# The down weights of an expert loop issued from ScalarE's queue instead of the first queue

## The chip, the cores and the metric

The kernel runs on one core of a Trainium2 chip. A core has TensorE (PE, matrix products; its weight loads are shown as PEld), VectorE (DVE), ScalarE (ACT), GpSimd (POOL) and SyncE (SP), each with a queue of its own, semaphores between them, and 16 DMA engines that carry what the queues issue. The metric is the device time of one execution in microseconds.

## The reference, cut to what matters

Two layers over 256 tokens of width 1024, all float32. Each layer is a mixer, a layer norm, a mixture of experts and another layer norm:

```
x = LN(alpha*x + mixer(x));  x = LN(alpha*x + MoE(x))
MoE(x): scores = sigmoid(x @ w_router)            # 64 experts, top 8 of each token
        routed = sum over chosen e of gate_e * (silu(x @ w_gate[e]) * (x @ w_up[e])) @ w_down[e]
        MoE = routed + (silu(x @ ws_gate) * (x @ ws_up)) @ ws_down
```

Of an expert, w_gate and w_up are 1024 x 256 and w_down is 256 x 1024, so each is 1 MiB; the 64 experts of a layer have 192 MiB, and each byte of them is read once.

## The kernel before, in words

The expert part works through 32 pairs of experts, four pairs (p = 0 to 3) to an octet, eight octets to a layer. For each octet the tokens of eight experts are gathered into columns by matmuls (L1916). For each pair PE runs `pe_pair`: gates and ups of both experts (L1945, 16 steps of two), half of the scatter of the pair before (L1995), the transposes of the hidden values and of the token map (L1967 to L1979), the other half of that scatter, for p = 3 the gather of the next octet, and the two halves of the down product (L1987). ACT (`act_pair`) makes silu (L2182), copies the token map (L2189), and for p = 3 half of the gathered columns, then waits for each half of the down product and copies it to `y_parts` as the high part (L2204). DVE makes the hidden product (L2276), its copy (L2282) and the low part (L2302).

The weights lie in five slots. Slots 0 and 1 (in `RING`) serve p = 0, slots 2 and 3 (in `AR`) serve p = 1 and p = 3, and p = 2 uses slot EX and slot 1 (EX has its gate and up weights in the first part of `RING` and its down weights in `GB`, where the norms' weights lie otherwise). A slot's gate and up part is free when `gate_up_done` says so, its down part when `down` does. In the last octet p = 2 uses slots 0 and 1, not EX.

All loads are issued by SP, in one written order, in `loads`. `load_experts(pair, experts)` waits for `gate_up_done` of the pair two before, issues the gate and up weights of its experts (`load_gate_up`, L1796 and L1797), waits for `down` of the same pair, and issues the down weights (`load_down`, L1800). In the first four octets the experts 8i+5 and 8i+8 go together, then 8i+6 and 8i+7, then 8i+9 and 8i+12, then 8i+10 and 8i+11. From the fifth octet on, `load_octet` takes 8i+8 after 8i+6 and 8i+7, and 8i+12 after 8i+10 and 8i+11. `load_last_pair` loads the last two experts, with the ups on a semaphore of their own. Behind it SP issues, in layer 0, the first weights of the next mixer (`load_rw`, into the places of slot EX, read by L1437), and in both layers the weights of the norm (`load_ln`, into `GB`, L459 and L460; in layer 1 first read by L422). PE waits for `gu_w[slot]` before a pair's gates and ups, and for `dn_w[slot]` before its down product.

Of the kernel before, what the change touches and what calls it, by code (L numbers as in the profile page):

```python
# [23 lines left out]
E = 64  # L24
# [9 lines left out]
PAIRS = E // 2  # L34
OCTS = E // 8
EX = 4
# [44 lines left out]
def program(nc, a):  # L81
    ctx = ExitStack()
    with ctx:
# [3 lines left out]
        def sem(name):  # L87
            return ctx.enter_context(nc.semaphore(name))
# [785 lines left out]
        def load_rw(sp, src, c):  # L874
            sp.dma_start(RWC[c].rearrange("p (k c) -> p k c", k=KT), src[:, :, c * CB:(c + 1) * CB]).then_inc(s_rw[c], 16)
# [663 lines left out]
        def pe_core(pe):  # L1539
# [231 lines left out]
        moe_shared = {n: sem("moe_" + n) for n in per_layer} | {  # L1771
            "gu_w": [sem(f"gate_up_loaded{s}") for s in range(EX + 1)],
            "dn_w": [sem(f"down_loaded{s}") for s in range(EX + 1)]}
        uses = [OCTS + 1, E // 4, E // 4, E // 4, OCTS - 1]
        gate_ups = [32 * n - (16 if s in (2, 3) else 0) for s, n in enumerate(uses)]
        once_an_octet = (0, EX)
        per_layer |= {"map_copied": PAIRS, "gates_ready": PAIRS, "turned": PAIRS + 1}
# [2 lines left out]
        def moe_view(l):  # L1780

            q = moe_shared | {n: sem(f"l{l}_{n}") for n in over_names}
            past = {n: l * count for n, count in per_layer.items()}
# [10 lines left out]
            def load_gate_up(sp, e, slot):  # L1794
                g, u, d = wslot(slot)
                sp.dma_start(g, gate_src(wg, e)).then_inc(q["gu_w"][slot], 16)  # L1796
                sp.dma_start(u, gate_src(wu, e)).then_inc(q["gu_w"][slot], 16)  # L1797

            def load_down(sp, e, slot):
                sp.dma_start(wslot(slot)[2], down_src(wd, e)).then_inc(q["dn_w"][slot], 16)  # L1800

            def load_expert(sp, e, slot):
                load_gate_up(sp, e, slot)
                load_down(sp, e, slot)
# [9 lines left out]
            def loads(sp):  # L1814
                sp.wait_ge(s_res, 2 * TT * st)
                if l == 0:
                    load_expert(sp, 0, 0)
                load_expert(sp, 2, 2)
                if l:
                    load_expert(sp, 3, 3)  # L1820
                g, u, d = wslot(EX)
                sp.wait_ge(s_ln, TT * (l + 1))
                load_down(sp, 4, EX)
                sp.wait_ge(q["shared_gate"], 1 + past["shared_gate"])
                sp.dma_start(g, gate_src(wg, 4)).then_inc(q["gu_w"][EX], 16)
                sp.wait_ge(q["shared_gate_up"], 1 + past["shared_gate_up"])
                sp.dma_start(u, gate_src(wu, 4)).then_inc(q["gu_w"][EX], 16)

                def load_experts(pair, experts):

                    sp.wait_ge(q["gate_up_done"], pair - 1 + past["gate_up_done"])
                    for e, s in experts:
                        load_gate_up(sp, e, s)
                    sp.wait_ge(q["down"], 2 * (pair - 1) + past["down"])
                    for e, s in experts:
                        load_down(sp, e, s)

                def load_last_pair():

                    sp.wait_ge(q["gate_up_done"], PAIRS - 2 + past["gate_up_done"])  # L1840
                    for e, s in ((E - 2, 2), (E - 1, 3)):
                        sp.dma_start(wslot(s)[0], gate_src(wg, e)).then_inc(q["gu_w"][s], 16)
                    for e, s in ((E - 2, 2), (E - 1, 3)):
                        sp.dma_start(wslot(s)[1], gate_src(wu, e)).then_inc(q["shared_and_last_ups_loaded"], 16)
                    sp.wait_ge(q["down"], 2 * (PAIRS - 2) + past["down"])
                    for e, s in ((E - 2, 2), (E - 1, 3)):
                        load_down(sp, e, s)

                def load_octet(i, twelfth):

                    load_experts(4 * i + 2, [(8 * i + 5, 1)])
                    load_experts(4 * i + 3, [(8 * i + 6, 2), (8 * i + 7, 3)])
                    load_expert(sp, 8 * i + 8, 0)
                    load_experts(4 * i + 4, [(8 * i + 9, 1)])
                    load_experts(4 * i + 5, [(8 * i + 10, 2), (8 * i + 11, 3)])
                    if twelfth == 0:
                        load_experts(4 * i + 6, [(8 * i + 12, 0)])
                    else:
                        load_expert(sp, 8 * i + 12, twelfth)

                sp.wait_ge(q["first_gates"], 1 + past["first_gates"])
                for e, s in ((5, 1), (8, 0)):
                    sp.dma_start(wslot(s)[0], gate_src(wg, e)).then_inc(q["gu_w"][s], 16)
                sp.wait_ge(q["gate_up_done"], 1 + past["gate_up_done"])
                for e, s in ((5, 1), (8, 0)):
                    sp.dma_start(wslot(s)[1], gate_src(wu, e)).then_inc(q["gu_w"][s], 16)
                sp.wait_ge(q["down"], 2 + past["down"])
                for e, s in ((5, 1), (8, 0)):
                    load_down(sp, e, s)
                load_experts(3, [(6, 2), (7, 3)])  # L1870
                load_experts(4, [(9, 1), (12, EX)])
                load_experts(5, [(10, 2), (11, 3)])
                with sp.Fori(1, 4) as i:
                    load_experts(4 * i + 2, [(8 * i + 5, 1), (8 * i + 8, 0)])
                    load_experts(4 * i + 3, [(8 * i + 6, 2), (8 * i + 7, 3)])
                    load_experts(4 * i + 4, [(8 * i + 9, 1), (8 * i + 12, EX)])
                    load_experts(4 * i + 5, [(8 * i + 10, 2), (8 * i + 11, 3)])
                with sp.Fori(4, OCTS - 2) as i:
                    load_octet(i, EX)
                load_octet(OCTS - 2, 0)  # L1880
                load_experts(PAIRS - 2, [(E - 3, 1)])
                load_last_pair()
                if l == 1:
                    load_ln(sp, st)
                else:
                    for c in range(2):
                        load_rw(sp, w_key, c)
                    sp.wait_ge(q["gate_up_done"], PAIRS)
                    for c in range(2, 4):
                        load_rw(sp, w_key, c)  # L1890
                    load_ln(sp, st)
                sp.wait_ge(q["rank_ready"], 1 + past["rank_ready"])
                most = nc.sync.value_load(cnti[0:1, 2 * l:2 * l + 1], min_val=0, max_val=T)
                with sp.If(most > CAP):

                    sp.wait_ge(q["over_list"], 1)
                    rounds = nc.sync.value_load(cnti[0:1, 2 * l + 1:2 * l + 2], min_val=1, max_val=NOV // 2)
                    with sp.Fori(0, rounds) as i:
                        sp.wait_ge(q["over_free"], i + 1)
                        for s in range(2):  # L1900
                            e = nc.sync.value_load(elist[0:1, ds(2 * i + s, 1)], min_val=0, max_val=E - 1)
                            g, u, d = wslot(s)
                            sp.dma_start(g, gate_src(wg, e)).then_inc(q["over_loaded"], 16)
                            sp.dma_start(u, gate_src(wu, e)).then_inc(q["over_loaded"], 16)
                            sp.dma_start(d, down_src(wd, e)).then_inc(q["over_loaded"], 16)
# [154 lines left out]
            def pe_moe(pe):  # L2060
# [54 lines left out]
                    for p in range(4):  # L2115
                        pe_pair(pe, 4 * i + p, p, i, True, spare=(p == 2))
                for p in range(4):
                    pe_pair(pe, PAIRS - 4 + p, p, OCTS - 1, False, last=(p == 3))
                pe.wait_ge(q["rank_ready"], 1 + past["rank_ready"])
                most = nc.tensor.value_load(cnti[0:1, 2 * l:2 * l + 1], min_val=0, max_val=T)  # L2120
                for n, made in enumerate(("high", "low")):
# [69 lines left out]
            def act_pair(s, i, p, oct_, more, last=False):  # L2191
                s.wait_ge(q["gate_up_done"], i + 1 + past["gate_up_done"])
                silu(q["silu_ready"])
                if not last:
                    s.wait_ge(q["gates_ready"], i + 2 + past["gates_ready"])
                    s.wait_ge(q["scattered"], i + past["scattered"])
                    copy_map(s, 1 - p % 2)
                if p == 3 and more:
                    for n in range(1, KT, 2):
                        wait_gathered(s, n, oct_ + 1)  # L2200
                        copy_gathered(nc.scalar.copy, n, oct_ + 1).then_inc(q["odd_copied"], 1)
                for h in range(2):
                    s.wait_ge(q["down"], 2 * i + h + 1 + past["down"])
                    nc.scalar.copy(YS[:, 0, h * 512:(h + 1) * 512], PS[:, 5 + h, :]).then_inc(q["high"], 1)  # L2204

            def residual(n):

# [359 lines left out]
```

## Time and profile before

| | us |
|---|---|
| median of 3 runs | 1322.86 (1322.58 to 1324.11) |
| the profiled execution | 1321.67 |
| its span | 1319.8 |
| PE busy in the span | 1300.7 (99%) |
| DVE, ACT busy | 441.5, 264.6 |
| HBM read | 448.26 MB, 340 GB/s over the span |

The expert loops lie from about 134 to 594 us and from about 846 to 1306 us. A busy time is the time in which the engine had an instruction under way; the ends of matmuls are modelled, so a busy PE isn't PE at its peak. In the chain of waits, a piece named "issue" is time in which PE waited for nothing that this view names; a landing of a DMA can lie behind it. A line such as `L1945` is a line of the kernel, printed above for the functions of the change.

### The profile page before, as it was taken

How to read it: one execution, taken by the hardware profiler on the slowest of the kernel's cores; microseconds unless marked ns; L12 is line 12 of the kernel's file. 1: busy time of each engine (PE TensorE's matmuls, PEld its weight loads, DVE VectorE, ACT ScalarE, POOL GpSimd, SP SyncE). 2: the span in 40 equal slices, each digit the busy share in tenths (PEclk: the TensorE clock that was granted, in tenths of full speed). 3: DMA queues.
4: the chain of work that ended last, by engine and by line, in shares of the span. 5: the costliest groups of instructions: out<-in, count | busy, mean ns of one | idle time of the engine just before them, and what ended most of it. 6: DMA issues, size and time to landing. Idle time of an engine off the chain costs nothing.

```text
span 1319.8 us, 23498 instructions
## 1 busy us (share of the span) xinstructions
PE 1300.7 (99%) x9812; PEld 753.2 (57%) x9812; DVE 441.5 (33%) x960; ACT 264.6 (20%) x524; POOL 79.8 (6%) x122
## 2 busy tenths in 40 slices
PE   9999999999999999999999999999999999999997
PEld 8889444435534443449688998734444353444433
DVE  2245122222222222228663665422223122222213
ACT  1231211111111111113432330211111111111111
POOL 7302000000000000000002201100000000000001
PEclk9999999999999999999999999999999999999999
DMA  5697799999999999995543016799999999999994
GB/s 184 162 383 318 295 423 415 422 422 422 422 416 422 422 422 422 421 391 173 188 158 101 4 43 270 313 384 418 422 421 423 421 422 415 422 422 422 422 421 179
DMA packets 98824, 450.38 MB, mean 341 GB/s; under 512 B 16193, under 2 KB 45505, under 8 KB 49089
## 3 DMA queue, kind: packets, MB, share of 16 engines
q1 hardware_dynamic: 98752, 449.34, 84.6%
q8 instruction: 56, 0.92, 0.3%
q14 instruction: 16, 0.12, 0.0%
HBM read 448.26 MB, written 1.05 MB: 340 GB/s over the span
## 4 chain that ended last, share of the span: by engine, by line
PE 95%; DVE 3%; ACT 1%; issue 1%; POOL 0%; DVEq 0%; POOLq 0%
PE PS L1945 31%; PE PS L1987 17%; PE PS L1995 10%; PE PS L1916 7%; PE PS L536 4%; PE PS L498 3%; PE PS L1412 2%; PE PS L1437 2%; PE PS L1398 2%; PE PS L1959 2%; PE PS L1967 1%; PE PS L1575 1%; PE PS L521 1%; PE PS L1591 1%; PE PS L2002 1%; PE PS L2071 1%
## 5 line engine op out<-in xcount | busy, mean ns | idle before, releaser
L2302 DVE TENSOR_TENSOR y_parts<-PS,y_parts 128x512 fp32r<-128x512 f32 x128 | 88.5, 692 | 216.5 <-ACT y_parts L2204 216.5
L2276 DVE SCALAR_TENSOR_TENSOR AR<-AR,PS 128x256 f32<-128x256 f32 x64 | 30.7, 480 | 382.7 <-ACT AR L2182 382.7
L1995 PE MATMUL PS<-y_parts,token_map 128*128 128x512 f32 x496 | 146.5, 417 | 0.0
L1995 PEld LDWEIGHTS PS<-y_parts,token_map 128*128 128x128 f32 x496 | 83.5, 188 | 60.0 <-issue 49.4
L1987 PE MATMUL PS<-AR 128*64 128x512 f32 x512 | 116.9, 598 | 0.0
L1987 PE MATMUL PS<-RING,AR 128*64 128x512 f32 x400 | 116.8, 598 | 0.0
L1945 PE MATMUL PS<-RING,xT 128*64 128x512 f32 x480 | 108.2, 592 | 1.6 <-issue 1.6
L2204 ACT CAST y_parts<-PS 128x512 fp32r<-128x512 f32 x128 | 75.0, 586 | 171.9 <-PE PS L1987 171.9
L1945 PE MATMUL PS<-AR,xT 128*64 128x512 f32 x480 | 108.2, 592 | 1.0 <-issue 1.0
L1945 PE MATMUL PS<-AR 128*64 128x512 f32 x480 | 108.1, 592 | 0.0
L1945 PE MATMUL PS<-RING,AR 128*64 128x512 f32 x480 | 108.1, 592 | 0.0
L2182 ACT ACTIVATE AR<-PS 128x256 f32<-128x256 f32 x64 | 24.6, 385 | 399.6 <-PE PS L1945 380.3
L1916 PE MATMUL PS<-slot_map,x_high 128*128 128x384 f32 x256 | 86.4, 337 | 0.1
L1916 PE MATMUL PS<-slot_map,x_low 128*128 128x384 f32 x256 | 85.8, 335 | 0.0
L1945 PEld LDWEIGHTS PS<-RING,xT 128*64 128x64 f32 x480 | 34.7, 137 | 70.3 <-issue 70.3
L1945 PEld LDWEIGHTS PS<-AR,xT 128*64 128x64 f32 x480 | 34.7, 137 | 69.8 <-issue 69.8
L1945 PEld LDWEIGHTS PS<-AR 128*64 128x64 f32 x480 | 35.0, 137 | 68.0 <-issue 68.0
L1945 PEld LDWEIGHTS PS<-RING,AR 128*64 128x64 f32 x480 | 34.9, 137 | 68.1 <-issue 68.1
L1987 PEld LDWEIGHTS PS<-AR 128*64 128x64 f32 x512 | 33.9, 136 | 64.8 <-issue 64.8
L1987 PEld LDWEIGHTS PS<-RING,AR 128*64 128x64 f32 x400 | 33.3, 136 | 38.1 <-issue 38.1
L2189 ACT CAST token_map<-PS 128x256 fp32r<-128x256 bf16 x64 | 23.8, 373 | 141.4 <-PE PS L1995 135.6
L1987 PE MATMUL PS<-GB,AR 128*64 128x512 f32 x112 | 51.1, 598 | 0.0
(329 smaller groups left out, 1553.5 us busy)
## 6 DMA issues: line engine op xcount, KB each, us to landing
RING<-in_moe_w_gate SPq DMA_DIRECT2D x64, 1024.0 KB, 12.2
RING<-in_moe_w_up SPq DMA_DIRECT2D x64, 1024.0 KB, 14.2
AR<-in_moe_w_gate SPq DMA_DIRECT2D x64, 1024.0 KB, 12.0
AR<-in_moe_w_up SPq DMA_DIRECT2D x64, 1024.0 KB, 14.1
AR<-in_moe_w_down SPq DMA_DIRECT2D x64, 1024.0 KB, 12.3
RING<-in_moe_w_down SPq DMA_DIRECT2D x50, 1024.0 KB, 14.1
GB<-in_moe_w_down SPq DMA_DIRECT2D x14, 1024.0 KB, 16.2
AR<-in_ab_w_in SPq DMA_DIRECT2D x16, 512.0 KB, 4.5
```

The costliest lines, as they stand in the source:

```text
L498: ins = nc.tensor.matmul(PS[:, 4 + 2 * b + c, 0:T], chunk(b)[:, k, c * P:(c + 1) * P], x[:, k, :], start=(k == 0), stop=(k == KT - 1))
L536: ins = nc.tensor.matmul(PS[:, 2 * t + c // 2, (c % 2) * CB:(c % 2) * CB + CB], x[:, k, t * P:(t + 1) * P], weights[c][:, k * CB:(k + 1) * ...
L1398: ins = mm(PS[half_rows[h], 4 + n % 4, 0:T], w[:, k, j * P + h * HD:j * P + (h + 1) * HD], swapped(x[:, k, :]) if h else x[:, k, :], start ...
L1412: ins = mm(heads_of(PS[half_rows[q], 4 + (2 * c + t) % 4, 0:CB])[:, :, h, :], x[:, k, n:n + CH], heads_of(w[:, k, :])[:, :, h, :], start=( ...
L1437: ins = mm(PS[half_rows[h], 2 * t + n // 4, (n % 4) * P:(n % 4) * P + P], w[:, k, (n % 2) * P + h * HD:(n % 2) * P + (h + 1) * HD], x.rear ...
L1916: ins = nc.tensor.matmul(PS[:, gather_bank(part, oct_), 0:8 * CAP], XP[n][:, t, part, :], SELR[:, t, :, :].rearrange("p s b -> p (s b)"), ...
L1945: ins = nc.tensor.matmul(PS[s * B:(s + 1) * B, 4, :], gathered(k)[:, c:c + B], gate_and_up(slots[s])[:, k, :, :], start=(k == 0), stop=(k ...
L1987: ins = nc.tensor.matmul(PS[s * B:(s + 1) * B, bank, :], HT[:, f, s * B:(s + 1) * B], wslot(slots[s])[2][:, f, h * 512:(h + 1) * 512], sta ...
L1995: ins = nc.tensor.matmul(PS[:, 2 * t + h, :], OHT[:, half, t, :], YS[:, n, h * 512:(h + 1) * 512], start=False, stop=True, skip_group_chec ...
L2204: nc.scalar.copy(YS[:, 0, h * 512:(h + 1) * 512], PS[:, 5 + h, :]).then_inc(q["high"], 1)
L2276: nc.vector.scalar_tensor_tensor(out=HH[0:2 * B, :].rearrange("p (k j) -> p k j", k=FT), in0=by_row(SIL[0:2 * B, :]), scalar=GC[:, buf:buf ...
L2302: nc.vector.tensor_tensor(YS[:, 1, h * 512:(h + 1) * 512], PS[:, 5 + h, :], YS[:, 0, h * 512:(h + 1) * 512], ALU.subtract).then_inc(q["low ...
```

## The change

ScalarE issues the down weights, in `act_pair`, behind the second of its two copies of the down product; SP's queue keeps gate and up weights alone in the loop. The first five experts' downs are still loaded by SP. SP no longer waits for `down` between the groups; it waits once, behind the last pair's loads, for the gates, ups and downs of pair 30, before it goes on to the next weights into the places of slot EX. The last octet's p = 2 uses slot EX as in the other octets, so expert 60 goes there.

```diff
--- before.py
+++ after.py
@@ -1771,7 +1771,7 @@
         moe_shared = {n: sem("moe_" + n) for n in per_layer} | {
             "gu_w": [sem(f"gate_up_loaded{s}") for s in range(EX + 1)],
             "dn_w": [sem(f"down_loaded{s}") for s in range(EX + 1)]}
-        uses = [OCTS + 1, E // 4, E // 4, E // 4, OCTS - 1]
+        uses = [OCTS, E // 4, E // 4, E // 4, OCTS]
         gate_ups = [32 * n - (16 if s in (2, 3) else 0) for s, n in enumerate(uses)]
         once_an_octet = (0, EX)
         per_layer |= {"map_copied": PAIRS, "gates_ready": PAIRS, "turned": PAIRS + 1}
@@ -1826,14 +1826,11 @@
                 sp.wait_ge(q["shared_gate_up"], 1 + past["shared_gate_up"])
                 sp.dma_start(u, gate_src(wu, 4)).then_inc(q["gu_w"][EX], 16)
 
-                def load_experts(pair, experts):
+                def load_gate_ups(pair, experts):
 
                     sp.wait_ge(q["gate_up_done"], pair - 1 + past["gate_up_done"])
                     for e, s in experts:
                         load_gate_up(sp, e, s)
-                    sp.wait_ge(q["down"], 2 * (pair - 1) + past["down"])
-                    for e, s in experts:
-                        load_down(sp, e, s)
 
                 def load_last_pair():
 
@@ -1842,21 +1839,15 @@
                         sp.dma_start(wslot(s)[0], gate_src(wg, e)).then_inc(q["gu_w"][s], 16)
                     for e, s in ((E - 2, 2), (E - 1, 3)):
                         sp.dma_start(wslot(s)[1], gate_src(wu, e)).then_inc(q["shared_and_last_ups_loaded"], 16)
-                    sp.wait_ge(q["down"], 2 * (PAIRS - 2) + past["down"])
-                    for e, s in ((E - 2, 2), (E - 1, 3)):
-                        load_down(sp, e, s)
-
-                def load_octet(i, twelfth):
-
-                    load_experts(4 * i + 2, [(8 * i + 5, 1)])
-                    load_experts(4 * i + 3, [(8 * i + 6, 2), (8 * i + 7, 3)])
-                    load_expert(sp, 8 * i + 8, 0)
-                    load_experts(4 * i + 4, [(8 * i + 9, 1)])
-                    load_experts(4 * i + 5, [(8 * i + 10, 2), (8 * i + 11, 3)])
-                    if twelfth == 0:
-                        load_experts(4 * i + 6, [(8 * i + 12, 0)])
-                    else:
-                        load_expert(sp, 8 * i + 12, twelfth)
+
+                def load_octet(i):
+
+                    load_gate_ups(4 * i + 2, [(8 * i + 5, 1)])
+                    load_gate_ups(4 * i + 3, [(8 * i + 6, 2), (8 * i + 7, 3)])
+                    load_gate_up(sp, 8 * i + 8, 0)
+                    load_gate_ups(4 * i + 4, [(8 * i + 9, 1)])
+                    load_gate_ups(4 * i + 5, [(8 * i + 10, 2), (8 * i + 11, 3)])
+                    load_gate_up(sp, 8 * i + 12, EX)
 
                 sp.wait_ge(q["first_gates"], 1 + past["first_gates"])
                 for e, s in ((5, 1), (8, 0)):
@@ -1864,22 +1855,20 @@
                 sp.wait_ge(q["gate_up_done"], 1 + past["gate_up_done"])
                 for e, s in ((5, 1), (8, 0)):
                     sp.dma_start(wslot(s)[1], gate_src(wu, e)).then_inc(q["gu_w"][s], 16)
-                sp.wait_ge(q["down"], 2 + past["down"])
-                for e, s in ((5, 1), (8, 0)):
-                    load_down(sp, e, s)
-                load_experts(3, [(6, 2), (7, 3)])
-                load_experts(4, [(9, 1), (12, EX)])
-                load_experts(5, [(10, 2), (11, 3)])
+                load_gate_ups(3, [(6, 2), (7, 3)])
+                load_gate_ups(4, [(9, 1), (12, EX)])
+                load_gate_ups(5, [(10, 2), (11, 3)])
                 with sp.Fori(1, 4) as i:
-                    load_experts(4 * i + 2, [(8 * i + 5, 1), (8 * i + 8, 0)])
-                    load_experts(4 * i + 3, [(8 * i + 6, 2), (8 * i + 7, 3)])
-                    load_experts(4 * i + 4, [(8 * i + 9, 1), (8 * i + 12, EX)])
-                    load_experts(4 * i + 5, [(8 * i + 10, 2), (8 * i + 11, 3)])
-                with sp.Fori(4, OCTS - 2) as i:
-                    load_octet(i, EX)
-                load_octet(OCTS - 2, 0)
-                load_experts(PAIRS - 2, [(E - 3, 1)])
+                    load_gate_ups(4 * i + 2, [(8 * i + 5, 1), (8 * i + 8, 0)])
+                    load_gate_ups(4 * i + 3, [(8 * i + 6, 2), (8 * i + 7, 3)])
+                    load_gate_ups(4 * i + 4, [(8 * i + 9, 1), (8 * i + 12, EX)])
+                    load_gate_ups(4 * i + 5, [(8 * i + 10, 2), (8 * i + 11, 3)])
+                with sp.Fori(4, OCTS - 1) as i:
+                    load_octet(i)
+                load_gate_ups(PAIRS - 2, [(E - 3, 1)])
                 load_last_pair()
+                sp.wait_ge(q["gate_up_done"], PAIRS - 1 + past["gate_up_done"])
+                sp.wait_ge(q["down"], 2 * (PAIRS - 1) + past["down"])
                 if l == 1:
                     load_ln(sp, st)
                 else:
@@ -2115,7 +2104,7 @@
                     for p in range(4):
                         pe_pair(pe, 4 * i + p, p, i, True, spare=(p == 2))
                 for p in range(4):
-                    pe_pair(pe, PAIRS - 4 + p, p, OCTS - 1, False, last=(p == 3))
+                    pe_pair(pe, PAIRS - 4 + p, p, OCTS - 1, False, last=(p == 3), spare=(p == 2))
                 pe.wait_ge(q["rank_ready"], 1 + past["rank_ready"])
                 most = nc.tensor.value_load(cnti[0:1, 2 * l:2 * l + 1], min_val=0, max_val=T)
                 for n, made in enumerate(("high", "low")):
@@ -2202,6 +2191,10 @@
                 for h in range(2):
                     s.wait_ge(q["down"], 2 * i + h + 1 + past["down"])
                     nc.scalar.copy(YS[:, 0, h * 512:(h + 1) * 512], PS[:, 5 + h, :]).then_inc(q["high"], 1)
+                if p < 2 or more:
+                    for n, slot in (((8, 0), (5, 1)), ((6, 2), (7, 3)), ((9, 1), (12, EX)), ((10, 2), (11, 3)))[p]:
+                        if p or n == 5 or more:
+                            load_down(s, 8 * oct_ + n, slot)
 
             def residual(n):
```

## Rows read from the trace of the kernel before

**Rows 1.** Page, 40 slices: mean busy share of the DMA engines in tenths.

```profile
DMA  5697799999999999995543016799999999999994
```

**Rows 2.** Windows: us, busy of each engine (instructions), PE clock, DMA share, GB/s.

```profile
164.00:172.00 8.00, 8.00 (x42) 3.39 (x39) 2.50 (x7) 0.76 (x2) 0.00 (x0) 1.00 1.01 425
299.52:358.04 58.52, 57.99 (x282) 26.38 (x281) 14.45 (x31) 9.64 (x20) 0.00 (x0) 1.00 1.01 422
415.82:473.61 57.79, 57.79 (x282) 26.03 (x281) 14.45 (x31) 9.64 (x20) 0.00 (x0) 1.00 1.01 422
```

**Rows 3.** Waits of PE: us in total, times, longest.

```profile
PE PS L1945 <- issue: 2.6, 4, 0.8
```

**Rows 4.** Chain of waits, layer 0: start us, us, what.

```profile
232.28 6.87 PE PS L1945 x32
...
290.05 6.87 PE PS L1945 x32
...
347.81 0.53 issue
...
521.93 6.87 PE PS L1945 x32
...
566.67 0.80 issue
567.47 7.09 PE PS L1945 x32
```

**Rows 5.** Timeline of SP's queue: start us, us, line, transfer, count.

```profile
214.65 0.38 SPq L1797 DMA_DIRECT2D AR<-in_moe_w_up  x1
219.26 0.81 SPq L1800 DMA_DIRECT2D AR<-in_moe_w_down  x2
...
272.42 0.38 SPq L1797 DMA_DIRECT2D AR<-in_moe_w_up  x1
...
330.19 0.38 SPq L1797 DMA_DIRECT2D AR<-in_moe_w_up  x1
...
504.04 0.43 SPq L1797 DMA_DIRECT2D AR<-in_moe_w_up  x1
```

**Rows 6.** DMA issues at 214.65, 272.42, 330.19, 504.04, in order: us to landing last.

```profile
AR<-in_moe_w_up SPq DMA_DIRECT2D x1, 1024.0 KB, 14.3
...
AR<-in_moe_w_up SPq DMA_DIRECT2D x1, 1024.0 KB, 16.2
...
AR<-in_moe_w_up SPq DMA_DIRECT2D x1, 1024.0 KB, 18.1
...
AR<-in_moe_w_up SPq DMA_DIRECT2D x1, 1024.0 KB, 16.0
```

**Rows 7.** DMA issues, windows 168.3:168.5 and 168.7:168.8; DMA queues, window 170:176.

```profile
RING<-in_moe_w_gate SPq DMA_DIRECT2D x1, 1024.0 KB, 6.8
...
RING<-in_moe_w_up SPq DMA_DIRECT2D x1, 1024.0 KB, 10.1
...
q8 instruction: 1, 0.02, 1.1%
```

**Rows 8.** DMA issues, window 387.2:387.4; landings of all issues of L1796.

```profile
AR<-in_moe_w_gate SPq DMA_DIRECT2D x1, 1024.0 KB, 5.7
...
DMA to landing us min/median/max: 4.6/12.2/19.1
```

**Rows 9.** Timelines of ACT (idle before it in brackets) and of SP's queue.

```profile
413.26 0.38 ACT L2182 ACTIVATE AR<-PS 128x256 f32<-128x256 f32 x1 [6.28 <-PE PS L1945]
...
1267.27 1.00 SPq L1797 DMA_DIRECT2D RING<-in_moe_w_up  x1
```

**Rows 10.** DMA issue at 1280.3, timeline of DVE, chain of waits.

```profile
GB<-in_ln_ffn_g SPq DMA_DIRECT2D x1, 512.0 KB, 18.2
...
1310.59 0.74 DVE L422 SCALAR_TENSOR_TENSOR X<-PS,mv,GB 128x512 f32<-128x512 f32 x1
...
602.50 7.14 PE PS L1437 x128
```

## The prediction

> **What bounds the kernel now.** The page's slices come first [rows 1]: TensorE (PE) is busy nearly throughout at full clock, and in two long stretches, the expert loops of the two layers, the DMA line reads 9 in every slice at some 422 GB/s. So there are two candidates. The table by octet (eight experts, four pairs) separates them [rows 2]: an undisturbed octet takes 57.79 us with PE busy for all of it, the fourth octet of the layer takes 58.52 us with 57.99 busy, and in both the DMA engines' share is full (1.01). The waits of PE [rows 3] hold only 2.6 us in four idle stretches before a gate-and-up group (L1945), none over 0.8 us, and the chain of waits [rows 4] shows two of them in layer 0: 0.53 us at 347.81 and 0.80 us at 566.67. Layer 1 has the other two. Both ends of each wait can be laid beside a landing. The last up weight of the pair that PE is ready for at 347.81 is issued at 330.19 [rows 5] and lands 18.1 us later [rows 6], at 348.3: PE waited for that transfer.
>
> The rate follows from the same rows. The last up of pair 7 (pairs count from 0) lands at 214.65 + 14.3 = 228.95, that of pair 27 at 504.04 + 16.0 = 520.04 [rows 5, 6]. Between them lie five octets of 24 transfers, less three (the loads of the slot-0 expert, which from octet 4 on come after those of pair 3): 117 transfers of 1 MiB in 291.1 us, 2.488 us each. An octet's 24 transfers thus take 59.7 us where PE needs 57.8: PE starts with a lead, and it shrinks by 1.9 us an octet. The slack of the last up before its pair shows it: pair 7 is ready at 232.28 and the up is there at 228.95 (3.3 us), pair 11 at 290.05 against 272.42 + 16.2 = 288.62 (1.4 us), pair 15 at 347.81 against 348.3 (0.5 us late), pair 27, after the gentler order of the later octets, at 521.93 against 520.04 (1.9 us) [rows 4 to 6]. The kernel is bound by PE with DMA full and just in time; what decides is the order in which transfers are served.
>
> **The change part by part.**
>
> Taken off SP: the 59 down loads of each layer behind the first five experts' (those five stay), with their waits for "down". Their issue costs SP 0.33 to 0.43 us each and nothing was late for SP itself, so this alone is worth 0.
>
> Put on ScalarE (ACT): mostly two issues a pair, behind the second high copy. By SP's rows they cost some 0.8 us a pair; ACT is idle for 6.28 us before the next silu [rows 9], so they are covered. If an issue stalls, as one of SP's did in the loop for 1.00 us [rows 9], it is still covered; only beyond 5.5 us would silu, then the hidden product, then the pair's turn on PE come late. The release moves by the copy's issue, under 0.7 us, against landings 10 us and more after issue: 0.
>
> Order within SP's queue: gates and ups no longer stand behind a wait for "down". In octets 0 to 3 their release (gate_up_done) is the same as before, so they come no earlier. From octet 4 on, the gates and ups of the slot-0 expert and of the slot-EX expert are released 6 us earlier, but still behind those of pair 3. In the last octet expert 60 goes to slot EX and is loaded one pair earlier; that takes away the wait at pair 30, 0.80 us plus the 0.22 us by which the group after a wait is longer (7.09 against 6.87) [rows 4]: -1.0 us a layer.
>
> Service of two loaded queues: this is the large term, and no row of before has two loaded queues of weights. The nearest: instruction fetches run on a queue of their own, and one that moved 0.02 MB (q8) in the stretch 170 to 176 us was served in the middle of a weight backlog of over 7 us: the transfers issued at 168.3 to 168.5 and 0.4 us later land 6.8 and 10.1 us later [rows 7], 3.7 us apart instead of 2.49. So a packet of another queue isn't made to wait behind the first queue's backlog; it cuts in and the first queue pays. I take equal turns between two loaded queues. The bounds: served in order of issue (nothing cuts in), or downs always first. A third possibility, the downs last, is a rival below.
>
> With equal turns: the gates and ups of pair 7 are issued up to 214.65, the two downs of the same experts at 219.26 [rows 5], when three of the four transfers still stand in SP's queue (they land from 224 to 228.95). Today the downs come behind them; after, both downs are served before the last of the three. The last up lands 2 x 2.488 = 4.98 us later, at 233.9: pair 7 is 1.6 us late. DMA stays full, so pair 11's up lands at 288.62 + 4.98 = 293.6 (3.5 us behind today's 290.05) and pair 15's at 353.3 (5.5 us behind 347.81). The delay isn't three times 4.98, since each landing is late by the same 4.98: PE loses its lead sooner and then runs at the rate of the queue, 59.7 us an octet.
>
> In octets 4 to 6 the down of the slot-0 expert also comes in ahead of pair 3, so three transfers cut in, 7.46 us. And DMA now has a pause it does not have today: the gate issued at 387.27 lands 5.7 us later [rows 8] where 4.6 us is the least that any load of that line took [rows 8], so the queue is only 1.1 us from empty. With PE 5.0 us later than today and one more transfer of 2.5 us that fills part of it (the slot-0 expert's down, which today comes after this gate) the pause is 5.0 - 1.1 - 2.5 = 1.4 us. Pair 27's up then lands at 520.04 + 7.46 + 1.4 = 528.9 against 521.93 today: 7.0 us, plus 0.2 us for the group after a wait. From there on no later pair is late (pair 30 is ready at 566.67 + 7.2 = 573.9; its last up, 567.4 today by the chain, would land at 567.4 + 1.4 + 2.5 = 571.3).
>
> Tails of the layers: SP now waits for the downs of pair 30 before the next weights. In layer 1 the norm's weights are issued at 1280.3 today and land 18.2 us later, behind the last experts' loads; they are first read at 1310.59 [rows 10]. Issued 13 us later into a nearly empty queue they land at about the same distance behind the last weights, over 8 us before their use: 0. If that cover were gone the cost would be the excess alone. In layer 0 the two w_k chunks move in the same way, with the queue still full until the last downs have landed, and L1437 first reads them at 602.50 [rows 10]: 0.
>
> Sum of a layer: +7.0 + 0.2 - 1.0 = +6.2 us; two layers, whose waits match [rows 3], +12.4 us. The profiled execution took 1321.67 us (span 1319.8, 1.9 around it), which gives 1334.1; it lies 1.2 us under the median of the runs, 1322.86, which gives 1335.2.
>
> The page "DMA: Bandwidth & Descriptors" of the Trainium skill says in its section on queues, rings and completion order that each DMA engine goes round between the queue rows that have work, a whole packet at a time. The fetch in [rows 7] fits that, but is one packet, not a backlog; by that rule the sum stays +12.4 us.
>
> **Rivals.**
>
> A, one order of issue for both queues. For it: all loads use the same 16 engines. Against it: the fetch of [rows 7]. Then nothing cuts in at pairs 7, 11 and 15; at pair 27 only the slot-0 expert's down is ahead, 520.04 + 2.49 = 522.5, 0.6 us late (0.8 with the longer group), and pair 30 gains 1.0. Net -0.2 us a layer: 1322.5. No change.
>
> B, two queues move more bytes than one. For it: the rate of one queue, 2.488 us a transfer, is only what one queue reaches. Against it: the engines' share is already full (1.01) [rows 2]. It decides where the 5.5 us by which pair 15 would be late are made up over the some 74 transfers of 2.488 us from 164 us, when the share is full [rows 2], to there: 0.074 us each, 3% (2.41 us). Then all four waits go, 2 x (0.53 + 0.22 + 0.80 + 0.22) = 3.5 us: 1319.3, faster. At 2.45 us the same sums leave about a third of the loss, 1327. The same page's section on issuing engines says that starting DMAs from several engines saves issue time alone, which speaks against this rival and leaves the sum as it is.
>
> C, unequal turns. If ACT's queue gets a third while both are full, which is its share of the bytes, fewer transfers cut in: about one instead of two, pair 15 is some 1 to 3 us behind today: 1325 to 1328. If it gets less than that, down weights become late instead, since four gates and ups go ahead of two downs; that costs what equal turns cost or a little more, up to 1340.
>
> D, ACT's issues block behind a full ring and silu comes late. Against it: ACT never has more than four loads outstanding, where SP has eight and more and loses at most 1.00 us. Each blocked pair would cost the part over 5.5 us. 1336 and more.
>
> **How the numbers follow.** Equal turns 0.62, at 1335 (its own range 1331 to 1338). A 0.15 and the mild end of C 0.08, 1322 to 1328. B 0.12. The other end of C and D 0.03. Under 0.2% (2.6 us) a measurement of this kernel can't tell a change. Slower: 0.62 + 0.03 + 0.06 = 0.71; same: A and a little of C, 0.17; faster: B, 0.12. The range takes in A and C, and leaves B's best and the costliest cases out: 1321 to 1338.
>
> **What would show it.** Right: PE waits before L1945 at pairs 7, 11, 15 and 27 of each layer of 1 to 2 us each; downs landing 5 to 8 us after their issue, last ups 5 us later than today against their issue; octets of 59.7 us from the second on; DMA bytes per second unchanged at 422; no wait at pair 30. Wrong: a last up of pair 7 that lands 14 us after its issue as today (A), a transfer time of 2.45 us or less (B), idle PE before L1987 (C), ACT's silu starting later than 0.2 us behind L1945 (D).

## The result, and the profile after

| | before | changed |
|---|---|---|
| median of the runs, us | 1322.86 | 1335.91 (5 runs, 1334.28 to 1337.71) |
| profiled execution | 1321.67 | 1334.28 |
| its span | 1319.8 | 1332.5 |
| ratio | 1 | 1.0096, 95% interval 1.0085 to 1.0106 |

The change makes the kernel 1.0% slower; the forecast was 1335 us, and 1334.1 for the profiled execution. No work was added on PE (1301.8 us busy against 1300.7). The waits of PE say where most of the 12.7 us of span went. In rows of the changed kernel L1934 is what was L1945, L1905 the gather, L1948 the last pair's gates. The row answers [rows 3] (us in total, times, longest):

```profile
PE PS L1934 <- issue: 13.7, 8, 2.1
```

Eight waits of 13.7 us in all stand where four of 2.6 us were: 11.1 us, with 0.9 us for four more groups that are longer behind a wait (7.09 us for 6.87), and 0.6 us in the second mixer, of which more below. The chain of waits of layer 0 gives their places and lines up with [rows 4] (start us, us, what):

```profile
232.22 1.22 issue
...
291.46 2.08 issue
293.54 7.09 PE PS L1934 x32
...
351.54 1.62 issue
...
526.77 2.09 issue
528.86 7.09 PE PS L1934 x32
...
573.81 6.87 PE PS L1934 x32
...
586.87 6.91 PE PS L1948 x64
...
853.20 7.06 PE PS L1948 x64
```

The waits stand before pairs 7, 11, 15 and 27. Pair 11 starts at 293.54 where it was 290.05 (+3.5), pair 15 at 353.16 (+5.3 on the 347.81 at which it was ready), pair 27 at 528.86 (+6.9 on 521.93). Pair 30 runs without a wait (573.81, 6.87 us). Layer 1 has waits before the same four pairs.

Why they are late is in SP's queue and in the landings of the same four last ups as [rows 5, 6], with the two downs issued at 219.35 and 219.86:

```profile
214.57 0.38 SPq L1797 DMA_DIRECT2D AR<-in_moe_w_up  x1
219.35 1.77 ACTq L1800 DMA_DIRECT2D AR<-in_moe_w_down  x2
```

```profile
AR<-in_moe_w_up SPq DMA_DIRECT2D x1, 1024.0 KB, 18.8
...
AR<-in_moe_w_down ACTq DMA_DIRECT2D x1, 1024.0 KB, 9.8
AR<-in_moe_w_down ACTq DMA_DIRECT2D x1, 1024.0 KB, 14.3
```

The last up of pair 7 lands at 214.57 + 18.8 = 233.4 instead of 228.95. The downs, issued 5 us behind it, land at 229.1 and 234.1: the first ahead of it, the second 0.8 us behind it and not two transfers behind. So the up is 4.4 us late, not quite the two whole transfers (4.98 us) of the sum. A closer look at four transfers of the stretch where both queues are loaded, two of each (the timelines, then the landings in the same order):

```profile
226.64 0.38 SPq L1797 DMA_DIRECT2D RING<-in_moe_w_up  x1
227.21 0.33 SPq L1796 DMA_DIRECT2D RING<-in_moe_w_gate  x1
...
232.41 0.34 ACTq L1800 DMA_DIRECT2D RING<-in_moe_w_down  x1
232.92 0.34 ACTq L1800 DMA_DIRECT2D GB<-in_moe_w_down  x1
```

```profile
RING<-in_moe_w_up SPq DMA_DIRECT2D x1, 1024.0 KB, 14.0
RING<-in_moe_w_gate SPq DMA_DIRECT2D x1, 1024.0 KB, 18.4
...
RING<-in_moe_w_down ACTq DMA_DIRECT2D x1, 1024.0 KB, 8.9
GB<-in_moe_w_down ACTq DMA_DIRECT2D x1, 1024.0 KB, 13.4
```

SP's two land at 240.6 and 245.6, ACT's at 241.3 and 246.3: each queue gets one transfer in 5.0 us, twice the 2.49 us of a queue alone. That is half the rate for each. The sum of both is unchanged, as the windows show (as [rows 2]: us, busy of the engines, clock, DMA share, GB/s; the first two are the octets that follow pair 7, from gather to gather, the third a later octet):

```profile
243.13:303.21 60.08, 58.00 (x282) 26.39 (x281) 14.45 (x31) 9.65 (x20) 0.00 (x0) 1.00 1.01 421
303.21:362.85 59.64, 58.02 (x281) 26.40 (x281) 14.45 (x31) 9.64 (x20) 0.00 (x0) 1.00 1.01 421
420.65:478.45 57.80, 57.80 (x282) 26.03 (x281) 14.45 (x31) 9.64 (x20) 0.00 (x0) 1.00 1.01 422
```

The two octets take 60.1 and 59.6 us, with PE idle for 2.1 and 1.6 us of them; the later one takes 57.8 us. In the octet between them lies the pause of DMA that the sum had laid out, before the gate that was issued at 387.27. The same stretch in the changed kernel, then in the one before:

```profile
385.00:395.00 10.00, 10.00 (x52) 4.05 (x50) 1.82 (x5) 1.34 (x3) 0.00 (x0) 1.00 0.83 313
385.00:395.00 10.00, 10.00 (x50) 4.11 (x48) 2.51 (x6) 1.93 (x4) 0.00 (x0) 1.00 0.99 404
```

With 313 GB/s instead of 404, some 2.2 us of transfers are not made in these 10 us, where the sum had 1.4.

### The profile page after: what moved, and what is told of

Same layout as the page of the kernel before. It is cut to its first block, busy times and chain, and to the rows that moved or that the text cites. A ratio compares the mean times of both kernels' runs of the same rounds, so it can differ in the third digit from the quotient of the medians.

```text
span 1332.5 us, 23616 instructions
## 1 busy us (share of the span) xinstructions
PE 1301.8 (98%) x9812; PEld 754.5 (57%) x9812; DVE 441.6 (33%) x960; ACT 264.6 (20%) x524; POOL 79.7 (6%) x122
## 3 DMA queue, kind: packets, MB, share of 16 engines
q10 hardware_dynamic: 16992, 123.74, 22.4%
## 4 chain that ended last, share of the span: by engine, by line
PE 94%; DVE 3%; issue 1%; ACT 1%; DMA 0%; POOL 0%; DVEq 0%; SPq 0%
PE PS L1934 31%; PE PS L1976 17%; PE PS L1984 10%; PE PS L1905 7%; PE PS L536 4%; PE PS L498 3%; PE PS L1412 2%; PE PS L1437 2%; PE PS L1398 2%; PE PS L1948 2%; PE PS L1956 1%; PE PS L1575 1%; PE PS L521 1%; PE PS L1591 1%; PE PS L1991 1%
## 5 line engine op out<-in xcount | busy, mean ns | idle before, releaser
L1934 PE MATMUL PS<-AR,xT 128*64 128x512 f32 x480 | 108.5, 593 | 13.7 <-issue 13.7
L1984 PEld LDWEIGHTS PS<-y_parts,token_map 128*128 128x128 f32 x496 | 83.5, 188 | 60.1 <-issue 49.5
L1934 PE MATMUL PS<-AR 128*64 128x512 f32 x480 | 108.3, 592 | 0.0
L1934 PE MATMUL PS<-RING,AR 128*64 128x512 f32 x480 | 108.1, 592 | 0.0
L1934 PE MATMUL PS<-RING,xT 128*64 128x512 f32 x480 | 108.1, 592 | 0.0
L1905 PE MATMUL PS<-slot_map,x_high 128*128 128x384 f32 x256 | 86.4, 338 | 0.1
L1905 PE MATMUL PS<-slot_map,x_low 128*128 128x384 f32 x256 | 85.8, 335 | 0.0
L1934 PEld LDWEIGHTS PS<-AR,xT 128*64 128x64 f32 x480 | 35.4, 137 | 83.1 <-issue 83.1
L1934 PEld LDWEIGHTS PS<-AR 128*64 128x64 f32 x480 | 36.3, 137 | 66.7 <-issue 66.7
L1934 PEld LDWEIGHTS PS<-RING,xT 128*64 128x64 f32 x480 | 34.5, 137 | 68.5 <-issue 68.5
L1934 PEld LDWEIGHTS PS<-RING,AR 128*64 128x64 f32 x480 | 34.5, 137 | 68.5 <-issue 68.5
L1976 PE MATMUL PS<-GB,AR 128*64 128x512 f32 x128 | 58.4, 598 | 0.0
## 6 DMA issues: line engine op xcount, KB each, us to landing
AR<-in_moe_w_up SPq DMA_DIRECT2D x64, 1024.0 KB, 12.9
GB<-in_moe_w_down ACTq DMA_DIRECT2D x14, 1024.0 KB, 13.7
```

Of the source, the lines that this page charges most:

```text
L1905: ins = nc.tensor.matmul(PS[:, gather_bank(part, oct_), 0:8 * CAP], XP[n][:, t, part, :], SELR[:, t, :, :].rearrange("p s b -> p (s b)"), ...
L1934: ins = nc.tensor.matmul(PS[s * B:(s + 1) * B, 4, :], gathered(k)[:, c:c + B], gate_and_up(slots[s])[:, k, :, :], start=(k == 0), stop=(k ...
L1976: ins = nc.tensor.matmul(PS[s * B:(s + 1) * B, bank, :], HT[:, f, s * B:(s + 1) * B], wslot(slots[s])[2][:, f, h * 512:(h + 1) * 512], sta ...
L1984: ins = nc.tensor.matmul(PS[:, 2 * t + h, :], OHT[:, half, t, :], YS[:, n, h * 512:(h + 1) * 512], start=False, stop=True, skip_group_chec ...
```

## The experiments

Ratios are to the kernel before, timed beside it on the same chip; "waits" are PE's before gate groups. The code cuts leave lines out, marked by three dots or said in brackets.

**The last octet alone.** Before, with slot EX in the last octet and SP's wait behind the last pair; all downs on SP.

```diff
-                load_octet(OCTS - 2, 0)
+                (Fori(4, OCTS - 1), every octet with EX)
+                sp.wait_ge(q["gate_up_done"], PAIRS - 1 + past["gate_up_done"])
+                sp.wait_ge(q["down"], 2 * (PAIRS - 1) + past["down"])
-                    ... last=(p == 3))
+                    ... last=(p == 3), spare=(p == 2))
```

> The change's last octet alone: pair 30 uses slot EX, SP waits for pair 30 before the next weights, all downs still on SP. Theory (the loss is made by two loaded queues taking equal turns): nothing is shared, so the loss is gone and the time is that of before, 1322.9, or 1 us a layer less if expert 60's earlier release is what took away the wait at pair 30 (1320.9). DMA is busy without a gap up to there, so an earlier release can't bring the last up of pair 30 forward: if that is so, pair 30 still waits about 0.8 us and the time is 1322.9. Rival (the last octet, or SP's new wait behind the last pair, makes a part of the loss): 1325 or more.

Measured: 1323.68 us, ratio 1.0003 (0.9992 to 1.0014). The waits are those of before, the one at pair 30 among them (the waits, then the chain, where L1943 is the line of the gates):

```profile
PE PS L1943 <- issue: 2.4, 4, 0.9
```

```profile
566.24 0.92 issue
567.15 7.09 PE PS L1943 x32
```

So this part costs nothing and brings nothing, and the earlier release of expert 60 does not end the wait at pair 30.

**Two queues alone.** The change with the last octet as before.

```diff
-                    load_gate_up(sp, 8 * i + 12, EX)
+                    if twelfth == 0:
+                        load_gate_ups(4 * i + 6, [(8 * i + 12, 0)])
+                    else:
+                        load_gate_up(sp, 8 * i + 12, EX)
...                            (and the rest of the last octet as in before)
```

> Downs on ACT's queue as in the change, the last octet as in before (expert 60 in slot 0, no new wait of SP). Theory: the whole loss is here, 1335 to 1336, with waits before the gates of pairs 7, 11, 15 and 27 of 1 to 2 us, and none at pair 30, since PE comes 6 us later there anyway. Rival (last octet makes a part): clearly under 1334.

Measured: 1336.61 us, 0.6 us over the expectation, ratio 1.0101 (1.0082 to 1.0119). The row of waits reads 14.1 us, 8 times, and pair 30 has none:

```profile
PE PS L1936 <- issue: 14.1, 8, 2.3
```

The two queues alone make the whole loss.

**Half of the bytes of the downs.** This kernel leaves out the second half of each down weight that ACT loads.

```diff
-                sp.dma_start(wslot(slot)[2], down_src(wd, e))
+                sp.dma_start(wslot(slot)[2][:, 0, :], down_src(wd, e)[:, 0, :])
```

> The change, but each down load of ACT carries only the first half of a down weight (0.5 MiB, the other half of the slot stays as it was), so an octet moves 20 MiB instead of 24 and DMA is no longer the limit; all instructions, queues and waits stay. Theory (PE waits because transfers of a full queue come late): no wait before any gates, 3.5 us under before: 1319.4. Rival (ScalarE's issues, or the handling of a second queue, cost PE or ACT time by themselves): stays well over 1322.9.

Measured: 1320.27 us where 1319.4 was expected, ratio 0.9980 (0.9969 to 0.9992), no wait before gates over 0.11 us, and an octet with DMA no longer full:

```profile
299.50:357.30 57.80, 57.80 (x282) 26.04 (x281) 14.45 (x31) 9.62 (x20) 0.00 (x0) 1.00 0.92 365
```

All of ACT's issues and the second queue are still there, so neither costs time by itself. The loss needs a full DMA.

**Downs one silu later.** The same loads, issued behind the silu of the next pair.

```diff
                 silu(q["silu_ready"])
+                if prior is not None and (prior[0] < 2 or prior[2]):
+                    (load_down of the pair before)
...
-                if p < 2 or more:
-                    (load_down of this pair)
```

> The change, but ACT issues a pair's downs behind the silu of the next pair, 6.9 us later. Theory of equal turns: the downs then cut in front of the gates and ups of the next pair as well and more transfers stand ahead of pair 7's last up when ACT's queue is loaded; laid out with 2.485 us a transfer and equal turns, pair 7 is 6.8 us late instead of 1.9 and the time is 14 to 15 us a layer over before: 1351 to 1353. Rival (the loss comes from downs issued too early, so a later issue mends it): under 1332, towards 1323.

Measured: 1365.10 us, ratio 1.0307 (1.0278 to 1.0336), 12 us over the expectation, and far from what "a later issue mends it" would give. The waits, and two of them in the chain with the gates behind them:

```profile
PE PS L1934 <- issue: 30.4, 12, 5.0
```

```profile
232.07 4.73 issue
236.81 8.78 PE PS L1934 x32
...
296.50 3.17 issue
299.67 9.93 PE PS L1934 x32
```

The waits alone are 30.4 us against 2.6, 27.8 us more, about the 28 to 30 us expected. The total fits better than the places: pair 7 waited 4.73 us, not 6.8, and other pairs make up for it. The rest is the clock: the gates behind a wait took 8.78 and 9.93 us where 7.09 are usual, and the second window, behind the wait, has half the clock, 1.2 GHz instead of 2.4; from 241 to 246 us it is full again:

```profile
229.00:236.00 7.00, 3.07 (x16) 0.76 (x12) 2.75 (x4) 1.17 (x2) 0.00 (x0) 1.00 1.02 424
237.30:240.60 3.30, 3.30 (x10) 1.20 (x8) 0.00 (x0) 0.00 (x0) 0.00 (x0) 0.50 1.00 417
```

The mean clock of this execution was 0.985, against 0.999 before: 1.4% of 1366 us, some 19 us, and 28 + 19 is about the 46 us of span that were added.

**Two queues in octets 0 to 3 alone**, timed twice, the second time beside the changed kernel, and **in the last octets alone**.

```diff
-                if p < 2 or more:
+                if downs:     (set for octets 0 to 3; in the other kernel from octet 4 on)
-                    load_gate_ups(4 * i + 2, [(8 * i + 5, 1)])
+                    load_experts(4 * i + 2, [(8 * i + 5, 1)])   (and so on, SP has the other downs)
```

> ACT issues the downs only behind the pairs of octets 0 to 3, SP those behind octets 4 to 6 in the order of before; last octet as in the change. Theory: pairs 7, 11 and 15 late as in the change (4.8 us a layer at pair 16), nothing cuts in at pair 27, a small or no wait at pair 30: +4 to +4.3 us a layer, 1331 to 1331.5. Rival (the cost is per transfer issued on the second queue, some 0.1 us for each of 59): 32 of 59 a layer, +7 us in all, 1330, but spread over the pairs and not in waits at pairs 7, 11 and 15.

> ACT's downs in octets 0 to 3 alone, again. By its waits before gates (11.3 us against 13.7 in the change) and by the queue laid out for it, it should be 3 to 4 us under the change, 1331 to 1332, when both have as many stretches of half clock. Rival: no difference to the change, as the first timing had it (1335.6 against 1335.9), that is, the last octets cost nothing.

> The changed kernel again, beside the next one, for a comparison on one chip: 1334 to 1337, and in the profile 1.7 us more for each 3.4 us in which TensorE has half its clock.

> SP issues the downs behind the pairs of octets 0 to 3 in the order of before, ACT those behind octets 4 to 7. Theory (equal turns use up the lead of the gates and ups, once): pair 15 waits 0.5 us as before, then pairs 19, 23 and 27 are late by 1 to 2 us each, none at pair 30: +4.9 us a layer, 1332 to 1333. The parts don't add up: 4.2 (first octets alone) and 4.9 (last alone) against 6.1 together. Rival (a cost for each transfer on the second queue): 27 of 59 transfers, under half of the loss, 1328.

Measured: the first octets alone 1335.55 us, ratio 1.0090 (1.0071 to 1.0109), then 1333.75, ratio 1.0079 (1.0066 to 1.0092); the changed kernel beside the latter 1337.23, ratio 1.0098 (1.0083 to 1.0114); the last octets alone 1333.90, ratio 1.0075 (1.0061 to 1.0089). The first timing missed its expectation by 4 us. Its profiled execution had a mean clock of 0.995 against 0.999 before, 5 us of 1334, and its waits were 11.3 us, so by waits it was about as expected. In the repeat the distance to the changed kernel came out at 3.5 us, as expected, but the first octets lay 1.8 us over their range and the changed kernel 0.2 over its own. Nor is the distance all a matter of waits: in the two profiles of the repeat they were 12.4 and 13.6 us, 1.2 apart, and the mean clocks 0.997 and 0.995, which is 2.7 us. The last octets alone came 0.9 us over the range. They wait at pair 15 a little, then at pairs 19, 23 and 27 (10.7 us in all, eight waits):

```profile
348.83 0.32 issue
407.14 1.67 issue
466.81 1.65 issue
526.45 1.66 issue
```

The parts, +0.79% and +0.75%, add up to far more than the +0.98% of both. There is one lead to use up; when it is gone, an octet costs 59.7 us instead of 57.8, that is about 1.7 us of wait an octet, wherever it was lost. A price for each transfer on the second queue is ruled out by that (and by the half downs).

**Downs in two halves, by partition and by row.**

```diff
-                sp.dma_start(wslot(slot)[2], down_src(wd, e)).then_inc(q["dn_w"][slot], 16)
+                for h in range(2):
+                    rows = slice(64 * h, 64 * h + 64)                   (by partition, 8 KB rows)
+                    sp.dma_start(wslot(slot)[2][rows, :, :], down_src(wd, e)[rows, :, :]) ...
+                    sp.dma_start(wslot(slot)[2][:, h, :], down_src(wd, e)[:, h, :]) ...   (by row, 4 KB rows)
```

> The change, but each down load is two transfers, of 64 partitions with rows of 8 KB each, so every engine gets half as many rows a transfer and no row changes. If the turns are taken by whole transfers (what an engine has of one), ACT's queue gets one third of the bytes while both are loaded, only half as much cuts in, and the time is about 1325. If the turns are taken row by row (or by bytes), nothing changes: 1335 to 1336, with landings of last ups as in the change.

> The change, but each down load is two transfers of 128 partitions with rows of 4 KB, so a row is half as long and a transfer has half the bytes. Both kinds of turn, by transfer and by row, give ACT's queue one third while both are loaded: about 1325, plus what shorter rows cost in rate (1 to 2% on a third of the bytes would be up to 3 us a layer of lead). Turns by bytes: 1335 to 1336 or more. Read with the run of halves by partition: only if that stays at 1335 and this one falls are the turns taken row by row.

Measured: by partition 1734.37 us, ratio 1.3126 (1.3065 to 1.3187); by row 1339.57 us, ratio 1.0133 (1.0107 to 1.0159). Both missed. By partition, the traces show why: halves nearly alone on the engines (the first window; 245 of its 274 packets are ACT's) move at half rate, and both queues together at 246 GB/s (the second, where PE mostly waits and its mean clock is 0.64):

```profile
225.80:234.40 8.60, 8.60 (x45) 3.38 (x41) 1.26 (x3) 0.97 (x2) 0.00 (x0) 1.00 0.91 209
262.00:300.00 38.00, 8.60 (x32) 2.99 (x34) 2.67 (x4) 1.17 (x2) 0.00 (x0) 0.64 1.01 246
```

The time says nothing of turns, but the landings do. SP's two transfers of 1 MiB, issued at 246.35 and 246.93, and two of ACT's halves, issued at 252.77 and 253.43:

```profile
AR<-in_moe_w_up SPq DMA_DIRECT2D x1, 1024.0 KB, 32.0
AR<-in_moe_w_gate SPq DMA_DIRECT2D x1, 1024.0 KB, 39.7
...
AR<-in_moe_w_down ACTq DMA_DIRECT2D x1, 512.0 KB, 19.2
AR<-in_moe_w_down ACTq DMA_DIRECT2D x1, 512.0 KB, 23.0
```

SP lands one in 8.3 us, ACT one half in 4.4 us: two short transfers of one queue against one long one of the other, so a turn isn't a transfer. The profile also counts packets, and a large one is one row: the 118 downs that ACT issues in the changed kernel have 16992 packets, 144 each, which is 128 rows and 16 small ones; by partition they have 160 each, 2 x (64 + 16), by row 288 each, 2 x (128 + 16). In stretches where both queues are loaded (q1 is SP's, q10 ACT's; packets, MB, share), by partition from 270 to 286 us and by row from 243.7 to 251.3 us:

```profile
q1 hardware_dynamic: 276, 2.00, 53.4%
q10 hardware_dynamic: 284, 1.89, 48.4%
...
q1 hardware_dynamic: 289, 2.11, 66.6%
q10 hardware_dynamic: 289, 1.05, 34.7%
```

Both queues get as many packets, also where ACT's have half the bytes, so a turn isn't a number of bytes: turns are counted in rows. (In the changed kernel it was 298 and 279 from 236 to 246 us.) How many rows a turn has, one or a few, wasn't settled.

So by row ACT's queue got a third of the bytes, as laid out, and pair 7 waited 0.40 us instead of 1.22. But pairs 11 and 15 waited 2.20 and 2.29 us, and the waits came to 12.9 us in all, hardly less than the 13.7 of the changed kernel. The kernel moves 417 GB/s instead of 422, 0.7 us an octet with no slack, which can be a part of the reason; no run shows how large a part. Half the clock behind two of the waits adds 1.7 us each.

**One queue in a new order**, timed twice: before, with the later octets' order from octet 3 on, and the gates and ups of experts 60 and 61 ahead of both downs.

```diff
-                with sp.Fori(1, 4) as i:
+                with sp.Fori(1, 3) as i:
-                with sp.Fori(4, OCTS - 2) as i:
+                with sp.Fori(3, OCTS - 2) as i:
...
-                load_octet(OCTS - 2, 0)
-                load_experts(PAIRS - 2, [(E - 3, 1)])
+                load_octet(OCTS - 2, None)        (no load of 8i+12 in this octet)
+                load_experts(PAIRS - 2, [(E - 4, 0), (E - 3, 1)])
```

> Before with two changes of SP's order: the gentle order of an octet (slot 0's expert behind those of pair 3) begins with octet 3 instead of 4, and in the last octet the gates and ups of experts 60 and 61 both go ahead of the downs of both. Theory (the queue is full, so only its order counts): pair 15's last up comes 3 transfers earlier and pair 30's last up one transfer (2.5 us) earlier, so both waits of before go, 0.53 + 0.22 and 0.80 + 0.22 us a layer, 3.5 us in all: 1319.4, no wait before any gates in the loop. Rival (the lead used up in octet 3 is missing at the end): pair 30 waits 0.5 us or more again, gain under 2.5 us.

> The one-queue kernel with the new order, again, on whatever chip comes: no wait before gates in the loop, 2 to 3.5 us under before (0.15 to 0.27%), the interval of the ratio below 1. Rival (the first timing was luck of the half-clock stretches): ratio within 0.1% of 1.

Measured: 1321.22 against 1323.39, ratio 0.9983 (0.9973 to 0.9993), and 1321.37 against 1324.00, ratio 0.9984 (0.9975 to 0.9993). Of the two waits of a layer both are gone; the chain at pair 30 of the repeat:

```profile
566.66 0.01 issue
566.67 7.09 PE PS L1943 x32
```

The gain is 2.2 and 2.6 us of the 3.5 expected; why not all of it is open. It is the fastest version that does all the work.

## Why the prediction was right, step by step

Equal turns between two loaded queues, the step that carried the forecast, is what the trace shows: one transfer of each queue in 5.0 us. Pair 7 was to start 1.6 us late and did so by 1.2, pair 11 by 3.5 (3.5), pair 15 by 5.5 (5.3), pair 27 by 7.0 (6.9); the end of layer 0, +6.2, came at +6.1 (586.87 against 580.74). Rate: 421 to 422 GB/s, as before, so rival B falls; a down issued 5 us behind the last up of pair 7 landed 4 us ahead of it, so A falls; each queue landed a transfer in 5.0 us and PE never waited for downs, so C falls; ACT's silu follows the gates as before, with one pair of issues taking 1.77 us inside its idle time, so D falls. The half-bytes run and the last octet alone support the same by experiment. That the profiled execution came within 0.2 us of its forecast (1334.28 against 1334.1) is partly luck, since terms below were off in both directions.

What was wrong or lacking:

The term of -1.0 us, put down to expert 60's earlier release, had the right size and the wrong cause. The last-octet run has the release and keeps the wait; the two-queue run lacks it and loses the wait. Pair 30 waited for a queue that was full, so an earlier place in the release changed nothing; with PE 7 us later, the up simply is there. An earlier place in the order helps, as in the new order.

The two terms of pair 27 were off against each other. Three transfers cutting in were to cost 7.46 us and the pause 1.4. The pause was about 2.2 us, and the up still landed 8.8 us later than before (528.77 against 520.01), as the 8.9 of the sum; so what cut in cost less than three whole transfers, as at pair 7, where it was 4.4 us instead of 4.98.

The forecast that downs would land 5 to 8 us after issue was too low: the two of the row above took 9.8 and 14.3 us, since each shares the engines. "Last ups 5 us later against their issue" held only at pair 7 (4.5 us); later their issue moves with PE.

The tail of layer 0 and the second mixer took 0.6 us more (853.20 is 6.75 over before's 846.45, the loop's end 6.1). No term of the sum has it. A wait before L1638 is 0.3 us of it (0.80 us where it was 0.54), and the repeat of the changed kernel has that wait at 0.5 again; the rest is open.

The Trainium skill's page "DMA: Bandwidth & Descriptors", in its section on queues, rings and completion order, was cited for turns by whole packets. Between queues in turn, the trace agrees, with packets as this profile counts them, one row each; the runs in halves show that a turn is no whole transfer and no fixed number of bytes. For equal transfers with equal rows the sum is the same. The rule of its section on issuing engines, that starting DMAs from several of them saves issue time alone, agrees with the 422 GB/s.

## What to carry to other kernels

When DMA is full and the consumer just in time, a second queue adds no bandwidth; it replaces a written order of service by equal turns, row against row, and what was issued last in need cuts in front of what is due first. So compare landing with use for each kind of load, find the least slack, and keep the loads on one queue in the order of their deadlines. By the same reasoning a split could help only where the loads of the second queue are due first; no run here tried that. Behind the full queue of this kernel a moved release was worth nothing (1323.68 us against 1323.39), a moved place in the order 2.2 to 2.6 us.

## What the runs showed of the hardware that was not expected

A PE that has waited for about 2 us or more can find its clock halved behind the wait. Behind the waits of 4.73 and 3.17 us above, with a mean clock of 0.50 in the window, the gates took 1.7 and 2.8 us longer; behind the two waits of 2.1 us of the profiled changed kernel it did not happen. The length of the wait alone doesn't decide: the repeat of the changed kernel has it behind 1.96 us, the repeat of the first octets alone doesn't behind 2.62 us:

```profile
1248.23 1.96 issue
1250.19 8.78 PE PS L1934 x32
...
291.68 2.62 issue
294.30 7.09 PE PS L1944 x32
```

Nor do the loop's waits alone make such stretches: the first run of the new order, with no wait before gates, had two in the second mixer (mean clock 0.50 from 738.5 to 741.5 us and 0.52 from 775.5 to 778.5). So the spread of the changed kernel's runs, 3.4 us, can't be put down to its waits alone: five runs of the one before spread by 3.5.

Transfers onto 64 of the 128 partitions ran at 209 GB/s nearly alone, half of what full ones reach, and held up the other queue's as well (243 GB/s for both from 270 to 286 us): 31% for the whole kernel from a change of the shape of a third of its loads. It is the partitions and not the size of 512 KB, since halves by row have that size too and moved at 417 GB/s with the other queue.
